# Two modulation panels move from the down projection into the MLA heads, the first output panel is worked in among the last pair of heads, and each output panel has banks of its own

## The reference

```python
x = first_block(x, ...)            # its last line: x = x + (silu(gate) * up) @ w_down
for i in range(2):                 # layer 0: pooling branch, layer 1: MLA branch (last)
    shift, scale, gate = split(silu(c) @ ada_w[i] + ada_b[i], 3)        # 3 x 2048 values
    h_lat = rms_norm(x, pre_norm[i]) * (1 + scale) + shift
    h_ctx = the same of ctx, with c_ctx in the place of c
    y_lat, y_ctx = pool_branch(...)  or  mla_branch(...)   # the last layer needs no y_ctx
    x = x + gate * rms_norm(y_lat, post_norm[i])

def mla_branch:                    # 16 heads, 128 + 64 wide for q and k, 128 for v
    c_q, c_kv, k_r, g = split(h @ w_in, [512, 1024, 1088])
    q = rms_norm(c_q) @ w_uq;  k_nope, v = rms_norm(c_kv) @ w_ukv
    p = softmax((q_nope k_nope + rope(q_rope) rope(k_r)) * MLA_SCALE)
    y_lat = ((p @ v) * silu(g)) @ w_out            # 2048 x 2048
```

## Time and profile before

| | |
|---|---|
| median of three runs | 2324.95 us |
| profiled execution | 2320.34 us, of which its span 2318.5 us |
| TensorE busy | 2274.8 us, 98% of the span |
| VectorE busy | 1677.5 us, 72% |
| ScalarE busy | 1028.1 us, 44% |
| mean granted TensorE clock | 0.997 |
| moved by DMA | 430.33 MB, 186 GB/s |

### The profile page before, as it was taken

One profiled execution on the slowest core, in us unless ns is written; L12 is line 12 of the kernel. 1 busy time (PEld: TensorE's weight loads), 2 busy tenths in 40 slices (PEclk: granted clock), 3 DMA queues, 4 the chain that ended last, 5 costly groups with the idle time before them and its releaser, 6 DMA issues.

```text
span 2318.5 us, 30884 instructions
## 1 busy us (share of the span) xinstructions
PE 2274.8 (98%) x11041; PEld 1885.8 (81%) x11041; DVE 1677.5 (72%) x2394; ACT 1028.1 (44%) x1474; POOL 77.9 (3%) x113
## 2 busy tenths in 40 slices
PE   8999999999999999999999999999999899999997
PEld 6878888888888888777878888888888799999876
DVE  5479976688788887787879676667874778666644
ACT  5565655555555554344462222222322634544432
POOL 1022200000000000000000000000000000000000
PEclk9999999999999999999999999999999999999999
DMA  8966645667676676787856555555664367422243
GB/s 243 215 185 207 192 137 172 196 215 229 213 238 223 223 228 204 232 264 245 258 169 211 170 180 162 174 156 164 227 200 132 121 188 219 132 74 63 72 158 133
DMA packets 225945, 430.33 MB, mean 186 GB/s; under 512 B 13847, under 2 KB 38671, under 8 KB 224688
## 3 DMA queue, kind: packets, MB, share of 16 engines
q1 hardware_dynamic: 222112, 418.96, 58.1%
q10 hardware_dynamic: 3152, 9.83, 1.3%
q0 software_dynamic: 576, 0.14, 0.0%
HBM read 426.16 MB, written 2.72 MB: 185 GB/s over the span
## 4 chain that ended last, share of the span: by engine, by line
PE 74%; issue 17%; DVE 4%; DMA 3%; ACT 1%; DVEq 0%; POOL 0%; SPq 0%; ACTq 0%; POOLq 0%
PE ps L641 46%; PE ps L676 13%; PE ps L653 10%; DMA raw<-in_w_down 2%; DVE ada_acc L610 1%; DVE lo L579 1%; PE ps L2437 1%; PE ps L2333 1%; PE ps L690 1%; ACT hi L575 1%; DMA xres<-in_x 1%; DMA raw<-in_w_up 0%; PE ps L2197 0%; PE ps L830 0%; DVE ustage L1794 0%
## 5 line engine op out<-in xcount | busy, mean ns | idle before, releaser
L575 ACT ACTIVATE hi<-raw 128x1024 fp32r<-128x1024 f32 x604 | 634.3, 1060 | 943.8 <-PE ps L641 358.1
L579 DVE TENSOR_TENSOR lo<-raw,hi 128x1024 fp32r<-128x1024 f32 x604 | 731.1, 1223 | 396.2 <-ACT hi L575 393.4
L610 DVE SCALAR_TENSOR_TENSOR ada_acc<-raw,csil,ada_acc 128x512 f32<-128x512 f32 x720 | 493.3, 749 | 4.8 <-DMA raw<-in_ada_w 4.6
L641 PE MATMUL ps<-hi,h_hi 128*128 128x512 f32 x960 | 382.1, 398 | 0.4 <-DVE lo L579 0.4
L641 PE MATMUL ps<-hi,h_lo 128*128 128x512 f32 x960 | 378.8, 395 | 0.0
L641 PE MATMUL ps<-lo,h_hi 128*128 128x512 f32 x960 | 378.8, 395 | 0.0
L641 PE MATMUL ps<-hi,g 128*128 128x512 f32 x704 | 227.2, 398 | 9.1 <-DVE lo L579 9.0
L641 PEld LDWEIGHTS ps<-hi,h_hi 128*128 128x128 f32 x960 | 180.8, 188 | 44.2 <-DVE lo L579 3.5
L641 PEld LDWEIGHTS ps<-hi,h_lo 128*128 128x128 f32 x960 | 180.7, 188 | 42.3
L641 PEld LDWEIGHTS ps<-lo,h_hi 128*128 128x128 f32 x960 | 180.9, 188 | 40.7
L641 PEld LDWEIGHTS ps<-hi,g 128*128 128x128 f32 x704 | 132.5, 188 | 44.2 <-DVE lo L579 14.2
(11 more groups left out here) (328 smaller groups left out, 3428.4 us busy)
## 6 DMA issues: line engine op xcount, KB each, us to landing
raw<-in_ada_w SPq DMA_DIRECT2D x192, 512.0 KB, 4.3
raw<-in_w_up SPq DMA_DIRECT2D x176, 512.0 KB, 4.5
raw<-in_w_down SPq DMA_DIRECT2D x88, 512.0 KB, 5.0
raw<-in_w_in SPq DMA_DIRECT2D x84, 512.0 KB, 4.6
raw<-in_pool_w_in SPq DMA_DIRECT2D x64, 512.0 KB, 4.4
raw<-in_mla_w_in SPq DMA_DIRECT2D x56, 448.0 KB, 4.1
raw<-in_w_out SPq DMA_DIRECT2D x32, 512.0 KB, 3.7
raw<-in_pool_w_out SPq DMA_DIRECT2D x32, 512.0 KB, 4.6
```

The source lines that it names most:

```text
L575: act.activation(hi[:, to, :, :], raw[:, slot, :, :], ACT.Copy).then_inc(hi_split, 1 + ada)
L579: dve.tensor_tensor(lo[:, to, :, :], raw[:, slot, :, :], hi[:, to, :, :].bitcast(F32), ALU.subtract).then_inc(lo_split, 1)
L610: ins = dve.scalar_tensor_tensor(acc, raw[:, slot, k, :], csil[:, v, kt:kt + 1], acc, ALU.mult, ALU.add)
L641: mm = pe.matmul(ps[:, bank, 0:n], tokens(a, kt0 + k, tok), w[:, slot, k, col0:col0 + n], start=first and k == 0 and s == 0, stop=last and ...
```

## The change

- The down projection carries one modulation panel per turn instead of two (16 chunks and two `turn_ada` less). The panels after it are numbered two lower. The last two of the 24, panels 22 and 23, are loaded during the heads, by `load_heads_ada`, into `heads_raw`, space in `proj_l` that the ring does not use: one chunk of each panel per pair. `heads_ada` is two groups of four DVE instructions per pair, one ahead of `pair_kn_lo` and one behind `pair_q_lo`.
- After the last pair's scores PE turns the two panels; `out_part` puts chunks 0 to 4 of the first output panel among these turns and the last pair's probabilities and rows. The gates are turned there and not at the start of the heads. Output panel n has banks 2n and 2n + 1, and the waits on `yout_taken` are gone.
- The last output panel does its chunks 4 to 7 for the first token tile, then for the second. Mean, power and join are made per token tile, the joins in halves of 1024 columns, with a store of 512 KB for each half.
- `n_mla` has a mean and a power per token tile. `norm_shift_split` writes `lo` of its first group ahead of `hi` of the second. The norms of `c_q` and `c_kv` are spread: squares of `c_q` in the fourth panel, the rows of `c_kv` among the chunks of the fifth.
- Some semaphores are merged.

```diff
-DOWN_ADA = [2 * RING + m * (2 * FT // CK_T - 2 * RING - 2) // (2 * CH) for m in range(2 * CH)]
+DOWN_ADA = [2 * RING + m * (2 * FT // CK_T - 2 * RING - 2) // CH for m in range(CH)]
...
-ADA_POOL = ADA_DOWN + D // W
+ADA_POOL = ADA_DOWN + D // W // 2
...
+        heads_raw = [proj_l[:, m, 0:CK_T * W].rearrange("p (k n) -> p k n", k=CK_T) for m in range(PAIR)]
...
             for g in range(n.groups):
-                if g + 1 < n.groups:
+                if 0 < g < n.groups - 1:
                     high(g + 1)
...
+                if g == 0:
+                    high(1)
...
+            def load_heads_ada(i):
+                for m in range(PAIR):
+                    col0 = (ADA_HEADS + m - ADA_PANELS) * W
+                    sp.wait_ge(heads_ada_added, (i * PAIR + m + 1) * 2 * CK_T)
+                    sp.dma_start(heads_raw[m], t["ada_w_2"][1][bass.ds(i * CK_T * P, CK_T * P), col0:col0 + W]
+                                 .rearrange("(k p) n -> p k n", p=P)).then_inc(heads_ada_loaded[m], 16)
+            load_heads(0)
+            load_heads(1)
+            with sp.Fori(0, PAIRS - 2) as i:
+                load_heads_ada(i)
+                load_heads(i + 2)
...
-            norm_mean(dve, n_mla)
-            norm_apply(dve, n_mla)
+            norm_mean(dve, n_mla, 1)
+            for i in range(TT):
+                norm_apply(dve, n_mla, i)
...
+            def heads_ada(i, m):
+                dve.wait_ge(heads_ada_loaded[m], i * 16 + 16)
+                before = (i * PAIR + m) * 2 * CK_T
+                for k in range(CK_T):
+                    for v in range(2):
+                        acc = ada_acc[:, m, v, :]
+                        scalar = csil[:, v, bass.ds(i * CK_T + k, 1)]
+                        dve.wait_ge(heads_ada_added, before + v + 3 + 3 * CK_T * k)
...
+                            ins = dve.scalar_tensor_tensor(acc, heads_raw[m][:, k, :], scalar, acc, ALU.mult, ALU.add)
+                        ins.then_inc(heads_ada_added, 1)
...
                 pair_turned(i, (2, 3))
+                heads_ada(i + 1, 0)
                 pair_kn_lo(i + 1)
                 pair_gate(i, (2, 3))
                 pair_q_lo(i + 1)
+                heads_ada(i + 1, 1)
                 pair_out_lo(i)
...
+            def out_row(i):
+                total, mean, root = (v[:, i:i + 1] for v in y_stats[1])
+                yout_gated(1, D // W - 1, 2 * (D // W - 1), slice(i, i + 1))
+                dve.reduce_sum(total, panel_sums[:, i:i + 1, :], AX_X).then_inc(yout_summed[1], 1)
...
+                for half in range(2):
+                    sl = slice(half * D // 2, (half + 1) * D // 2)
+                    dve.scalar_tensor_tensor(xres[:, i, sl], YOUT[1][i][:, sl], root, xres[:, i, sl], ALU.mult, ALU.add)\
+                       .then_inc(yout_added[1], 1)
...
-            for ms in ((0, 1), (2, 3)):
-                pair_probs(PAIRS - 1, ms)
-                pair_rows(PAIRS - 1, ms)
+            for j in range(2):
+                turn_ada(pe, ADA_HEADS + j, j, 2)
+                out_part(0, j, pair(0))
+            pair_probs(PAIRS - 1, (0, 1))
+            out_part(0, 2, pair(0))
+            pair_rows(PAIRS - 1, (0, 1))
+            turn_gates(1, 3)
+            pair_probs(PAIRS - 1, (2, 3))
+            out_part(0, 3, pair(0))
+            pair_rows(PAIRS - 1, (2, 3))
+            out_part(0, 4, pair(0))
             pair_columns(PAIRS - 1)
...
+            for j in range(RING):
+                out_part(n, j, out_banks(n))
+            for j in range(RING, CH):
+                mm = out_part(n, j, out_banks(n)[0:1], False)
+            mm.then_inc(lat_summed, 1)
+            for j in range(RING, CH):
+                out_part(n, j, out_banks(n)[1:TT])
```

183 lines of the change are left out of this document (119 added, 64 removed).

## The result

The changed kernel takes 2298.75 us (median of four runs, 2297.67 to 2299.72) against 2323.87 us (2320.81 to 2325.65) for the kernel before beside it: ratio 0.9894, 95% interval 0.9880 to 0.9908. Forecast was 2301.4 with a range of 2292 to 2313. The profiled execution took 2297.67 us, its span 2295.9 us, 22.6 less than before's.

A forecast was written before the change was run, and what follows sets the result against it. PE, busy in 98% of the span, was taken to bound the kernel. Terms 11.8 + 1.8 + 1.6 + 1.4 - 0.7 + 4.2 + 3.4 = 23.5 us against the 2324.95 median gave 2301.4, range 2292 to 2313.

The forecast's parts named there:

- A: Rival: low clock stays at the MLA input's start, the last pair or both; costs 1.6 or 3.4 us; chance 0.17.
- C: Rival: in the heads `kn_lo` is late in each pair by up to 1.5 us, kernel at 2312; chance 0.09.
- D: Rival: DVE's added 5.3 us per pair of heads lands on PE's path, kernel slower at 2338 us; chance 0.03.
- the slack forecast at 0.25 us: Heads: first modulation group ends at 2085.0, `kn_lo` starts at 2085.28; each 0.1 us over costs 0.1 seven times.
- Down projection, 11.8 forecast: Down projection: 9.9 us of PE waits and restarts gained, plus 1.9 for two `turn_ada` and two switches leaving.
- I take 1.8 (1.5 of the first wait ...): Down projection: of 11.7 us of waits and restarts 1.8 stay, mostly the first wait, at the context load.
- the waits that come from density: Down projection: waits where transfers need 256 GB/s and the stage moves 249; should go at 222 GB/s.
- The row nearest to that is the wait of 2.10 us: MLA input's start: the 2.0 to 2.3 us left compare with a down projection wait where the clock stays 1.00.
- So I take 1.6 gained: MLA input's start: transposes and matmuls at 2.4 GHz instead of 1.2 gain 1.6 us, bounds 0 and 1.6.
- starts one power earlier, 0.70 us: MLA input's start: first tile's `norm_apply` starts 0.70 us earlier, both tiles ready 0.75 earlier; part of the 1.8 gain.
- Last pair: Last pair and output: last score to last matmul's start from 102.3 to 98.1 us, gain 4.2, bounds 0.9 and 6.
- End: After the last matmul: 12.3 us becomes 8.9, gain 3.4, taking 3.5 us for a store of 512 KB.

The follow-up runs named there:

- both groups ahead: Changed kernel with both groups of modulation work on VectorE ahead of the subtraction in each turn of the head loop: 2323.24 us.
- few bytes: Kernel before, each modulation load in the down projection bringing 4 of 512 columns, VectorE's work kept: 2312.70 us.
- few columns: Kernel before, VectorE's operations on modulation chunks in the down projection taking 16 of 512 columns, all bytes loaded: 2310.98 us.
- serial last pair: Changed kernel with the last pair and the first output panel one behind the other again, not interleaved: 2304.42 us.

## Why the prediction was right, and where its terms were off

**The mechanism** was right for the waits in each place, and no rival decided; for the clock it was not shown (below). In the profiled execution A's low clock came at neither of its two places, but at a third, behind the first wait of the down projection. C and D didn't happen: the slack forecast at 0.25 us is 0.25 us in the trace. The run with both groups ahead shows how near D was: 2.7 us of the same work at another place in the queue.

**The total.** The terms say 23.5, the profiles 22.6, of which 1.7 is a stretch of low clock in the profiled execution of before (below). The median nevertheless came out 2.65 lower than forecast: 1.1 is the median of before (2323.87 beside this run, 2324.95 in the forecast), 2.4 that the profiled execution of before lies 3.5 below its median and the one of after 1.1, less the 0.9 by which the terms were too high.

**Down projection, 11.8 forecast, 10.1 measured.** The failed step is "I take 1.8 (1.5 of the first wait ...)". The first wait kept 2.42 us, and with restart and clock 3.9. That the modulation chunk behind it would shorten it was an argument without a row. Its length isn't fixed either: in executions of the changed kernel's stage, unedited, it was 0.87 to 2.82 us. Second, "the waits that come from density" were reckoned in bytes, 256 against 249 GB/s; the runs with few bytes and few columns show DVE's work on the chunk as somewhat the larger part, and the second turn, as dense and without a wait in 117 us, shows that density needs something to set it off. That those waits go was right, because the change takes away both the bytes and DVE's work.

**The clock.** "The row nearest to that is the wait of 2.10 us" was taken to say that such idleness leaves the clock alone. One row doesn't say that: in the down projection the clock stayed behind 2.10 us and fell to half for some seven matmuls behind 2.17 to 2.82 us, in eight executions. Nor does the length of a wait decide it: elsewhere the clock stayed behind 2.75 us (serial last pair) and behind one of seven waits of 2.24 to 2.27 us in the heads. By the Trainium skill (TensorE: Matmul & The Clock Gate, "The HAM clock gate"), which the forecast weighed, idleness halves the clock; here the trace agrees that it can.

At the MLA input the failed step is "So I take 1.6 gained", as a gain of the change. The 1.6 came between the two profiled executions, but by luck. The start of the kernel before is in three traces: in the profiled one the clock fell at 1816.3, behind the waits, and the rest of the projection took 181.6 us; with few columns it fell at 1804.3, during the transposes, and with few bytes not at all, and the rest took 179.9 us in both. With the changed kernel's start, unedited, the clock held in seven of eight traces. How often it falls with either start, and so what the change is worth there, these traces don't say. At the last pair it is open too: the clock fell there in all three traces with the old order, and not in the run with the serial order.

**MLA start, 1.8 forecast, 1.0 measured.** The failed step is "starts one power earlier, 0.70 us". The powers became 1.46 and 1.53 us, because DVE's subtraction and the first tile's scaling ran beside them. The order of the first groups gave 0.7 where 1.05 was estimated. The Trainium skill has a rule that fits (SBUF — State Buffer, "SBUF: two separate sides"): GpSimd and a VectorE instruction that has two inputs in SBUF, or runs in a mode that uses two ports, share one pair of ports, and the later one waits for the other's whole instruction. The trace agrees: the powers end at 1797.80 and 1800.03, each 0.41 us behind DVE's instruction beside it. I had not weighed it.

**Fifth panel** 1.4 against 1.3; **heads** -0.7 against +0.1: no wait of PE in them came from the first pair's late modulation chunk. **Last pair** 4.2 against 5.2: the half microsecond for the second `turn_ada` was mostly not needed (0.1), and the rest is smaller switches than reckoned. **End** 3.4 against 4.2: a store of 512 KB takes 2.7 us where I took 3.5 (the forecast's terms add up to 8.8 us, not 8.9). The fit that the forecast takes from the Trainium skill (DMA: Bandwidth & Descriptors, "Anatomy of one DMA") is stated there for transfers that GpSimd issues; these stores are SyncE's, and took 2.7 us where it gives 3.2.

**Not tried**: the separate banks, and the banks of before within the changed kernel; that they give nothing rests only on no row showing PE waiting for `yout`. Nor was the kernel before tried with its context load moved.

## What to carry to other kernels

Ask of work moved to another engine not how busy that engine is but who waits behind it in the queue: the same 2.7 us were free behind one subtraction and cost 3.5 us per pair ahead of it. Where a ring feeds TensorE, issue a large side load when the ring is full, and try it in parts; issued while it refills, 2 MB cost 3.9 us. Before waits are put down to a stage's density, look whether they are spread over it: here nine of ten stood in one of two like turns. Price a wait at more than its row: the restart came on top and, behind most waits of over 2 us here, a stretch at half clock. And read a clock term from several executions: with the same code at the same place it came in one and not in another.

## What was unexpected in the hardware

- A power of one column on GpSimd takes 0.55 us with VectorE idle and 1.46 to 1.53 us beside a VectorE instruction of 1.2 to 1.3 us.
- In the down projection a wait shown as 2.17 to 2.42 us on PE costs 1.5 to 1.9 us more than that: the matmul ahead of it is followed 0.40 us later than the wait alone gives, instead of 0.23, and seven or so behind it are 0.43 us apart. A wait of 2.10 us and shorter ones there cost some 0.27 more.
- Behind the same three waits (1.16 to 1.17, 0.80, 1.83 us) TensorE's clock fell to half in one execution and stayed in another. A wait of 2.75 us left it alone elsewhere.
- The stores of 512 KB took 2.7 us, those of 1 MB 4.0.
